# Expert stage of a mixture-of-experts layer: 22 steps of four 32-slot blocks in four column groups of TensorE, in place of 33 blocks of 128 slots

## The reference, cut to what matters

```python
D_MODEL, N_GROUPS, EXPERTS_PER_GROUP, EXPERT_FF = 1024, 4, 4, 256
def hier_moe(h, lw):
    hf = h.reshape(-1, D_MODEL)
    ...
    g_idx = jnp.argmax(g_logits, axis=-1)
    ...
    top_l, top_i = lax.top_k(e_sel, TOP_K_IN_GROUP)
    weights = p_g * jax.nn.softmax(top_l, axis=-1)
    expert_ids = g_idx[:, None] * EXPERTS_PER_GROUP + top_i
    combine = jnp.sum(jax.nn.one_hot(expert_ids, N_EXPERTS) * weights[..., None], axis=1)
    hidden = (jax.nn.silu(jnp.einsum('nd,edf->nef', hf, lw['w_exp_gate']))
              * jnp.einsum('nd,edf->nef', hf, lw['w_exp_up']))
    y = jnp.einsum('nef,efd->nd', hidden * combine[..., None], lw['w_exp_down'])
```

## Time and profile before

| | us |
|---|---|
| median of 3 runs (1278.42 to 1280.49) | 1279.99 |
| span of the profiled execution | 1277.0 |
| routing stage, from its first instruction to the first of the expert stage | 848.6 to 874.9 |
| expert stage, first product to last product | 883.9 to 1216.1 |
| final stage | 1220.9 to 1277.0 |

### The profile page before, as it was taken

One profiled execution on the slowest core, in us unless ns is written; L12 is line 12 of the kernel. 1 busy time (PEld: TensorE's weight loads), 2 busy tenths in 40 slices (PEclk: granted clock), 3 DMA queues, 4 the chain that ended last, 5 costly groups with the idle time before them and its releaser, 6 DMA issues. The chain is left out here.

```text
span 1277.0 us, 19756 instructions
## 1 busy us (share of the span) xinstructions
PE 1155.7 (91%) x6190; PEld 964.7 (76%) x6190; DVE 825.9 (65%) x1268; ACT 666.7 (52%) x1118; POOL 262.3 (21%) x205
## 2 busy tenths in 40 slices
PE   4799999988999996988997999987999999999974
PEld 1687777768999885888886788886777778888751
DVE  0764455105465785776776466656889889999737
ACT  2651112113434773666666566413787888888622
POOL 0000000021000682467663000001111112111050
PEclk9899999999999997999999899987999999999987
DMA  9427686512200917245110623134977897842375
GB/s 357 147 105 266 200 281 228 152 48 59 55 1 1 215 50 169 49 105 126 44 67 1 201 100 131 68 117 141 348 269 263 304 344 258 304 153 99 117 260 216
DMA packets 127092, 204.93 MB, mean 160 GB/s; under 512 B 19264, under 2 KB 89824, under 8 KB 124974
## 3 DMA queue, kind: packets, MB, share of 16 engines
q1 hardware_dynamic: 118108, 176.90, 42.1%
q0 software_dynamic: 7344, 26.74, 6.0%
q10 hardware_dynamic: 1570, 0.38, 0.2%
HBM read 215.61 MB, written 45.01 MB: 204 GB/s over the span
## 5 line engine op out<-in xcount | busy, mean ns | idle before, releaser
L88 DVE TENSOR_TENSOR moe_wgu_lo<-moe_wgu,moe_wgu_hi 128x1024 fp32r<-128x1024 f32 x132 | 155.6, 1219 | 9.1 <-ACT moe_wgu_hi L2224 8.9
L2224 ACT CAST moe_wgu_hi<-moe_wgu 128x1024 fp32r x132 | 131.8, 1052 | 44.7 <-DMA moe_wgu<-in_w_exp_gate 23.6
L93 PE MATMUL proj_acc_ps<-proj_w_hi,hidden_hT_hi 128*128 128x512 f32 x288 | 117.6, 408 | 7.5 <-DVE hidden_hT_lo L88 7.5
L95 PE MATMUL proj_acc_ps<-proj_w_hi,hidden_hT_lo 128*128 128x512 f32 x288 | 114.3, 397 | 0.0
L94 PE MATMUL proj_acc_ps<-proj_w_lo,hidden_hT_hi 128*128 128x512 f32 x288 | 113.9, 396 | 0.0
L93 PE MATMUL moe_gu_ps<-moe_wgu_hi,moe_xT_hi 128*128 128x512 f32 x264 | 107.8, 408 | 3.1 <-DVE moe_xT_lo L88 3.1
L95 PE MATMUL moe_gu_ps<-moe_wgu_hi,moe_xT_lo 128*128 128x512 f32 x264 | 105.0, 398 | 0.0
L94 PE MATMUL moe_gu_ps<-moe_wgu_lo,moe_xT_hi 128*128 128x512 f32 x264 | 104.8, 397 | 0.0
L1350 ACT ACTIVATE att_e<-att_sc_ps,att_shift 128x1152 f32<-128x1152 f32 (+1 forms) x72 | 81.4, 1131 | 40.8 <-DVE att_shift L1401 40.7
L1332 POOL TENSOR_TENSOR att_e<-att_e 128x1152 f32<-128x1152 f32 (+1 forms) x36 | 86.0, 2389 | 73.8 <-DVE att_e L1412 73.8
L1401 DVE TENSOR_REDUCE att_shift<-att_sc_ps 128x1 f32<-128x1152 f32 (+1 forms) x72 | 86.2, 1231 | 5.6 <-PE att_sc_ps L1446 5.5
(11 more groups left out here) (381 smaller groups left out, 2820.5 us busy)
## 6 DMA issues: line engine op xcount, KB each, us to landing
moe_wgu<-in_w_exp_gate SPq DMA_DIRECT2D x34, 1024.0 KB
moe_wgu<-in_w_exp_up SPq DMA_DIRECT2D x34, 1024.0 KB
moe_wd<-in_w_exp_down SPq DMA_DIRECT2D x34, 1024.0 KB
scratch_y_slots<-moe_y SPq DMA_DIRECT2D x33, 512.0 KB
proj_raw<-in_w_in SPq DMA_DIRECT2D x32, 256.0 KB, 5.1
proj_feat<-in_w_ada SPq DMA_DIRECT2D x4, 2048.0 KB, 8.9
proj_xh<-in_w_ada SPq DMA_DIRECT2D x4, 2048.0 KB, 9.9
scratch_h<-late_h SPq DMA_DIRECT2D x9, 512.0 KB, 2.9
```

What stands on the lines that cost most here:

```text
L88: return eng.tensor_tensor(low, value, high.bitcast(F32), ALU.subtract)
L93: pe.matmul(out, a_high, b_high, start=start, stop=False)
L95: return pe.matmul(out, a_low, b_high, start=False, stop=stop)
L2224: act.copy(wgu_hi[:, k.buf, j:j + 2], wgu[:, buf, j:j + 2]).then_inc(gu_hi_done, 1)
```

## The change

The blocks become 32 slots wide, so the slots of an expert are filled up to a multiple of 32: at most 88 blocks. They are dealt to four streams of 22 in a row each: blocks 0 to 21 to stream 0, 22 to 43 to stream 1, and so on. Step n of 22 takes block n of each stream. The four blocks sit in four column groups of PE: the stationary operand is 32 columns of the turned rows, the output goes to partitions 32c to 32c+31, and the moving operand is the weights of stream c's own expert. The products are single plain fp32 matmuls; the splitting by ACT and DVE is gone, and so are the high and low copies.

Each stream has one buffer of weights (`wgu[:, c]`, `wd[:, c]`). SP reads eight registers per step (four experts, four conditions), then issues the gate and up loads of the first half, those of the second half, and the down loads, 20 in all, each under its condition. The store of the results moves from SP to ACT's queue and gets two buffers; the gather gets three. ACT and DVE each copy half of every PSUM tile. The routing stage loads the first experts of all four streams at its end, once `block_expert` is known. The loops are written out for all 22 steps.

With the numbers of pairs above, stream 0 takes a new expert at steps 5, 8, 12 and 16, stream 1 at 8, 13 and 19, stream 2 at 4, 8, 13 and 18, and stream 3 at 3 and 8.

```diff
+Q = 32
+STREAMS = P // Q
+BLOCKS = -(-(2 * TILES * P + NE * (Q - 1)) // (STREAMS * Q)) * STREAMS
+STEPS = BLOCKS // STREAMS
...
+def load_gate_up(sp, I, W, c, half, e, **cond):
+    rows = slice(half * (KT // 2), (half + 1) * (KT // 2))
+    for name, first in (("w_exp_gate", 0), ("w_exp_up", FF)):
+        sp.dma_start(W["wgu"][:, c, rows, first:first + FF], I[name][0, e].rearrange("(k p) f -> p k f", p=P)[:, rows], **cond
+                     ).then_inc(W["gu_in"][half], 16)
+def load_down(sp, I, W, c, e, **cond):
+    sp.dma_start(W["wd"][:, c], I["w_exp_down"][0, e].rearrange("(k p) d -> p k d", p=P), **cond).then_inc(W["d_in"], 16)
+def expert_of(eng, W, c, step):
+    n = c * STEPS + step
+    return eng.value_load(W["block_expert"][0:1, n:n + 1], min_val=0, max_val=NE - 1)
...
 routing_stage, sync:
-            sp.wait_ge(last_done, 1)
-            sp.dma_start(M["h2"][(TILES - 1) * P:, :], W["h2"][:, (TILES - 1) % 2]).then_inc(W["h2_in"], 16)
+            for half in range(2):
+                load_gate_up(sp, I, W, 0, half, 0)
+            load_down(sp, I, W, 0, 0)
+            sp.wait_ge(blocks_done, 1)
+            firsts = [expert_of(sp, W, c, 0) for c in range(STREAMS)]
+            other = is_new(sp, W, 0, 0)
+            for half in range(2):
+                sp.wait_ge(W["gu_in"][half], 16 * 2)
+                load_gate_up(sp, I, W, 0, half, firsts[0], cond=other)
+                for c in range(1, STREAMS):
+                    load_gate_up(sp, I, W, c, half, firsts[c])
...
 expert_stage, sync:
+            for n in range(1, STEPS):
+                experts = [expert_of(sp, W, c, n) for c in range(STREAMS)]
+                new = [is_new(sp, W, c, n) for c in range(STREAMS)]
+                for half in range(2):
+                    sp.wait_ge(gu_done[half], n)
+                    for c in range(STREAMS):
+                        load_gate_up(sp, I, W, c, half, experts[c], cond=new[c])
+                sp.wait_ge(d_done, n)
+                for c in range(STREAMS):
+                    load_down(sp, I, W, c, experts[c], cond=new[c])
...
 expert_stage, tensor:
+                pe.wait_ge(gu_in[half], gu_loaded(n))
+                for k in range(half * (KT // 2), (half + 1) * (KT // 2)):
+                    for c in range(STREAMS):
+                        at = slice(c * Q, (c + 1) * Q)
+                        mm = pe.matmul(gu_ps[n % 2][at, :], xT[:, n % 2, k * P + c * Q:k * P + (c + 1) * Q], wgu[:, c, k],
+                                       start=(k == 0), stop=(k == KT - 1))
+                mm.then_inc(gu_done[half], 1)
...
+            for n in range(STEPS):
+                if n + 1 < STEPS:
+                    gate_up(n + 1, 0)
+                turn_hidden(n)
+                if n + 2 < STEPS:
+                    turn_x(n + 2)
+                if n + 1 < STEPS:
+                    gate_up(n + 1, 1)
+                down(n)
```

More of the change, by code:

```diff
@@ L1983, in _ @@
             dve.drain()
-            tt(more[:], bcast(upto[:, :, T - 1], T, 2), bcast(starts[:, 0:T], NE, 1), ALU.is_gt)
+            dve.tensor_scalar(raised[:], upto[:, :, T - 1], float(Q - 1), None, ALU.add)
+            dve.drain()
+            dve.tensor_scalar(over[:], raised[:], Q - 1, None, ALU.bitwise_and)
             dve.tensor_tensor(place[:], upto[:], rank_ps[:, 0:T * NE].rearrange("p (e t) -> p e t", t=T), ALU.subtract)
-            dve.tensor_reduce(nblk[:], more[:], AX, ALU.add)
@@ new lines, in expert_stage, with gu_loaded, d_loaded @@
+        h_turned, hidT_done, d_done = s.sem("h_turned"), s.sem("hidT_done"), s.sem("d_done")
+        y_left, y_right, y_out = s.sem("y_left"), s.sem("y_right"), [s.sem(f"y_out{u}") for u in range(2)]
+        block = ctx.enter_context(nc.Block())
+        token, weight = W["step_token"], W["step_weight"]
+        left, right = slice(0, 512), slice(512, 1024)
+        first_loads = STREAMS + 1
+        def gu_loaded(n):
+            return 32 * (first_loads + STREAMS * n)
+        def d_loaded(n):
+            return 16 * (first_loads + STREAMS * n)
@@ L2207, in _, with down @@
-            keep_busy(pe, y_ps, ident, 14)
-            turn_x(Step(0, 0))
-            gate_up(Step(0, 0), 0)
-            turn_x(Step(0, 1))
-            gate_up(Step(0, 0), 1)
-            blocks(pe, body)
+            def down(n):
+                pe.wait_ge(hidT_done, n + 1)
+                pe.wait_ge(d_in, d_loaded(n))
+                if n >= 1:
+                    pe.wait_ge(y_left, n)
+                    pe.wait_ge(y_right, n)
+                for cols in (left, right):
+                    for j in range(2):
+                        for c in range(STREAMS):
+                            at = slice(c * Q, (c + 1) * Q)
+                            mm = pe.matmul(y_ps[at, cols], hidT[:, j * P + c * Q:j * P + (c + 1) * Q], wd[:, c, j, cols],
+                                           start=(j == 0), stop=(j == 1))
+                mm.then_inc(d_done, 1)
@@ new lines, in silu, with y_half, store @@
+            def silu(n):
+                act.wait_ge(gu_done[1], n + 1)
+                if n >= 1:
+                    act.wait_ge(hid_done, n)
+                act.activation(act_g[:], gu_ps[n % 2][:, 0:FF], ACT.Silu).then_inc(silu_done, 1)
+            def y_half(n):
+                act.wait_ge(d_done, n + 1)
+                if n >= 2:
+                    act.wait_ge(y_out[n % 2], 16 * (n // 2))
+                act.copy(y[:, n % 2, left], y_ps[:, left]).then_inc(y_left, 1)
+            def store(n):
+                act.wait_ge(y_left, n + 1)
+                act.wait_ge(y_right, n + 1)
+                act.dma_start(M["y_slots"][n * P:(n + 1) * P, :], y[:, n % 2]).then_inc(y_out[n % 2], 16)
@@ L2286, in _ @@
+            x_out(0)
+            x_out(1)
+            silu(0)
+            for n in range(STEPS):
+                if n >= 1:
+                    y_half(n - 1)
+                    store(n - 1)
+                if n + 2 < STEPS:
+                    x_out(n + 2)
+                if n + 1 < STEPS:
+                    silu(n + 1)
+            y_half(STEPS - 1)
+            store(STEPS - 1)
+            for u in range(2):
+                act.wait_ge(y_out[u], 16 * ((STEPS - u + 1) // 2))
         @block.vector
@@ L2533, in build @@
         W["final_in"] = e.sem("final_in")
-        W["wgu"], W["wd"] = e.sb("wgu", [P, 2, KT, 2 * FF]), e.sb("wd", [P, 2, 2, D])
+        W["gu_in"], W["d_in"] = [e.sem(f"gu_in{half}") for half in range(2)], e.sem("d_in")
+        W["wgu"], W["wd"] = e.sb("wgu", [P, STREAMS, KT, 2 * FF]), e.sb("wd", [P, STREAMS, 2, D])
         routing_stage(nc, I, C, W, M)
```

439 lines of the change are left out of this document (140 added, 299 removed).

## The result

The changed kernel takes **1500.05 us** (median; 1498.28 to 1501.89) against 1279.2 us of the kernel before, run on the same chip. The ratio is 1.1728, with a 95% interval of 1.1706 to 1.1749. The forecast was 1494 us, in a range from 1449 to 1550. The profiled execution has a span of 1496.4 us.

The account below looks back on a forecast made before the run. PE was taken to bound the expert stage. Start 919, 20 cycles of 23.0 us (460), moved loads 47 and the last step's 4.5 gave 1430.5; with the end and 3.0 for the runs' median, 1494 us, range 1449 to 1550.

Parts of the forecast that it names:

- PE's work: Expert stage: 12 groups of four matmuls, 10 transposes and form changes take 11.7 us a step, 258 for 22 steps.
- the rule of the Trainium skill: Rival in the expert stage: weight loads sharing a row group stand in the open, adding 211 us, about 1705; chance 3%.
- The gap: Heads of steps 2 to 21: PE idles 8.5 us while SP issues down loads, register loads, then gate and up pairs.
- The clock: PE restarts after each of 20 gaps at a lower clock, losing 2.8 us of work each; bounds 1.7 and 5.8.
- Moved loads: Steps that load new experts' weights: PE waits longer, 47 us together, bounds 25 and 75.
- The start: Routing stage's 9 MiB of first loads delay the expert stage by 12 us: first product at 896, step 0 done at 919.
- The end: Last product to final stage: 4.9 us less 0.5 for the halved copy; the final stage itself: 56.1 us.
- The rival "not slower": PE doesn't wait at the head of a step: 1255 us, 2% faster; decided by a 1.25 us gap; chance 4%.

Follow-up runs that it names:

- The kernel with the gap removed: Changed kernel with SP's down loads of step n, and their wait, moved behind the registers, gate and up loads of step n+1: 1283.49 us.
- the kernel with the registers two steps ahead: Kernel with down loads behind the next step's, with registers of step n+2 read behind the half 1 loads of step n+1: 1281.09 us.
- The final version: Kernel with first loads on two queues, with SP's eight register loads of step n+2 spread between other loads instead of together: 1268.27 us, ratio 0.9943.
- the kernel with the filled gap: Changed kernel with 30 unread identity products on PE ahead of the wait for weights at each head from step 2 on: 1468.43 us.
- the kernel with the first experts fixed: Registers-two-steps-ahead kernel with first experts of streams 1 to 3 written as numbers and loaded at the head of the routing stage: 1281.84 us.
- the start split: Registers-two-steps-ahead kernel with only half 0's first loads in the routing stage, half 1 and down loads at the expert stage's head: 1282.18 us.

## Why the prediction was right, step by step

- **PE's work**: 11.7 us a step forecast, 11.68 measured over 19 steps. The price of a group of four, taken from two calls of another stage, held for 264 groups. By the rule of the Trainium skill that I had weighed ("TensorE: Matmul & The Clock Gate", Part 3, "The mechanism") weight loads into the same row group would stand in the open; the trace disagrees: in the 221.92 us of the window above PE's products leave no gap, while 77.75 us of weight loads run beside them.
- **The gap**: 8.5 forecast, 7.84 measured. The chain was named rightly, and taking its two causes away showed it: without SP's wait for the down products in front of the loads, the gap is gone; without the registers in it, 2.85 stay. Of its parts, register loads were 4.6 forecast and 5.0 measured, pairs 2.4 and 2.1, down loads 0.8 and 0.57. I had rounded up for slow register loads, and those came about once in each set.
- **The clock**: 2.8 forecast, 1.6 to 3.0 measured for a restart, 2.4 on average over the 20 steps. Filling the rest with products gave the full clock back where it reached to within 2.2 us of the end of the rest.
- **Moved loads**: the term that was mis-sized, 47 forecast and 68 measured. The seven single steps cost 4.0 to 6.0 each, where I had 2.3 to 4.1: I priced the pair by one load of 512 KB landing in 3.9 us. In step 12 the gate load was issued at 1181.64, the up load at 1182.13, and PE began at 1187.50, 5.4 us behind the second. The window of that wait:

```profile
1182.00:1187.50 5.50, 0.00 (x0) 0.03 (x1) 0.00 (x0) 0.00 (x0) 0.00 (x0) 0.50 0.80 257
```

  That is 1.4 MB, the 1.05 of the pair and a part of the next half's, which SP issued from 1184.45 on. When each of the two landed the trace doesn't say. The seven sum to 35.5 against 23; step 13 cost 8.3 (6), step 8 17.8 (18), and 6 were spread over heads without loads, most of them right behind such steps, which I had not counted.
- **The start**: the first product came at 895.8 (896), D(0) ended at 917.3 (919). Half the reason was right: SP's issues, slow with many loads ahead of them (2.48 us for one, 2.98 for the four down loads), hold the barrier; freeing it gave 5 to 6 us. That they are the whole 12 us was wrong: the bytes and the gather follow close behind.

These rows of the changed kernel show the held issues and the gather behind the barrier:

```profile
872.61 2.48 SPq L1853 DMA_DIRECT2D moe_wgu<-in_w_exp_up  x1
...
881.52 2.98 SPq L1858 DMA_DIRECT2D moe_wd<-in_w_exp_down  x4
886.29 1.15 POOL L2124 DMA_INDIRECT moe_xg<-scratch_h,all_step_token  x1 [36.88 <-POOLq L86]
```

- **The end**: from the last product to the final stage 6.1 us (4.4 forecast), and the final stage 58.3 (56.1 forecast). Together 4 us; why was not tried.

```profile
1438.12 7.34 PE L104 MATMUL fin_unread_ps<-all_ident 128*128 128x128 f32 x48 [6.08 <-PEq L86]
```

- **The rival "not slower"** had its place and its point of decision: its 1255 us were for no gap at all. The kernel with the gap removed took 1283, since the moved loads that I let it hide by half cost more: 59 us and not 34 in the kernel with the registers two steps ahead. The final version shows the other side: the change as an idea isn't slower; its order on SP is.

That the sum comes within 6 us of the time is in part luck: gaps and clock were 20 us too high, loads 21 too low.

## What to carry to other kernels

Ask of every wait on an issuing queue what stands behind it, register loads and loads that move nothing included: 20 times 7.84 us of a sequencer's work, which no busy share shows, undid a gain of 75 us of PE's work. When the engine that was the bound gets faster, price its rests too: of the rests of 2.85 us or more at a head here, three were free, and all others that were the only wait of their burst cost 1.4 to 3.0 us of clock. Loads into a single buffer can start only when its last reader is done, so issue each at that moment and put the sequencer's own work (registers, loads of other tiles) into the times in which it waits anyway.

## What the runs showed of the hardware

- A load under a false condition costs SP 0.07 us of issue, 0.17 with its MOVE and gaps, and PE started 0.12 us behind the last of them.
- A register load with its check costs SP 0.55 us; in steps without loads, one in most sets of eight took 0.6 us more, and a second set read at once added no slow one.
- Behind a rest of 2.85 us the granted clock fell to 1.2 GHz within 1 us of PE's restart in three of five cases (bursts of 13.4 to 13.6 us for 11.9); behind the eleven rests of 0.8 to 2.2 us in the kernel with the filled gap it never did. But rests of 2.11 and 2.21 us in the kernel with the first experts fixed were followed by bursts of 13.58 us, so rests of 2.1 to 2.9 us ended both ways.
- Four column groups with four different moving operands kept 11.68 us a step for 222 us, to the hundredth, while DMA moved 84 GB/s.
- SP's issue of one 512 KB load took 0.38 to 0.46 us with little ahead of it. With many loads ahead it took up to 2.5 us in the changed kernel, 3.1 with the first experts fixed, 4.4 with the start split, and 4.6 when the scalar engine issued loads beside it.
